# The output product of two attention mixers: native float32 or three rounded products

## The reference

```
def sliding_sink_attention(h, w_in, w_out, sinks, rel_table):
    q, k, v = jnp.split(h @ w_in, [qw, qw + kw], axis=-1)
    ...
    o = banded_attention(q, k, v, rel_table, A_WINDOW, sinks)
    return o.reshape(B, S, -1) @ w_out
```

## Time and profile before

| | |
|---|---|
| median of three runs | 2666.44 us (2665.11 to 2669.57) |
| the profiled execution | 2662.52 us, of which the span of the trace is 2660.7 |
| PE busy | 2609.0 us, 98% of the span |
| DVE, ACT, POOL busy | 1745.3, 1293.1, 241.9 us |
| first mixer A, steps 0 to 9 | from 239.0 to 291.3 us |
| fourth mixer A, steps 0 to 9 | from 1778.7 to 1831.0 us |
| granted PE clock | 0.99 over the span, 1.00 in both mixers A |

### The profile page before, as it was taken

How to read it: one execution, slowest core, us unless ns; L and a number is a source line. 1 busy time by engine, 2 the same in 40 slices (tenths; PEclk the granted TensorE clock), 3 DMA queues, 4 the chain that set the end, 5 groups by cost and what they waited for, 6 DMA issues and landing times.

```text
span 2660.7 us, 37977 instructions
## 1 busy us (share of the span) xinstructions
PE 2609.0 (98%) x13576; PEld 2103.9 (79%) x13576; DVE 1745.3 (66%) x2589; ACT 1293.1 (49%) x2041; POOL 241.9 (9%) x364
## 2 busy tenths in 40 slices
PE   8999999999998999999999999999999999899999
PEld 7887688888874788888988888886888654688887
DVE  6764577777674777777567777745776542577776
ACT  5444454544544544545565454435443221466665
POOL 0001100100111100101110010012001001000000
PEclk9999999999998999999999999999999999999999
DMA  9542555454332555453355545434553222478885
GB/s 321 193 148 87 180 207 189 153 204 179 116 115 82 219 191 192 151 189 141 135 183 215 192 169 190 158 135 150 194 197 132 95 95 71 178 276 287 302 299 191
DMA packets 337248, 472.40 MB, mean 178 GB/s; under 512 B 15632, under 2 KB 275056, under 8 KB 337152
## 3 DMA queue, kind: packets, MB, share of 16 engines
q1 hardware_dynamic: 334464, 464.02, 48.9%
q0 software_dynamic: 2192, 6.94, 0.8%
q10 hardware_dynamic: 496, 0.17, 0.0%
HBM read 470.01 MB, written 1.10 MB: 177 GB/s over the span
## 4 chain that ended last, share of the span: by engine, by line
PE 90%; DVE 5%; ACT 2%; issue 1%; DMA 1%; POOL 0%; SPq 0%; DVEq 0%; ACTq 0%; POOLq 0%
PE psum_all L1456 22%; PE psum_all L1460 12%; PE psum_all L1508 6%; PE psum_all L1509 6%; PE psum_all L1510 6%; PE psum_all L1593 4%; PE psum_all L2455 4%; PE psum_all L1718 3%; PE psum_all L3396 3%; PE psum_all L3415 3%; PE psum_all L3392 3%; PE psum_all L3393 2%; PE psum_all L1635 2%; PE psum_all L3420 1%; PE psum_all L2577 1%
## 5 line engine op out<-in xcount | busy, mean ns | idle before, releaser
L1456 PE MATMUL psum_all<-hT_both,gu_hi 128*128 128x512 f32 x2688 | 670.8, 391 | 0.3 <-DVE gu_lo L1286 0.3
L1456 PEld LDWEIGHTS psum_all<-hT_both,gu_hi 128*128 128x128 f32 x2688 | 492.8, 188 | 95.5 <-DVE gu_lo L1286 0.6
L1286 DVE TENSOR_TENSOR gu_lo<-raw_ring,gu_hi 128x2048 fp32r<-128x2048 f32 x176 | 402.1, 2286 | 15.1 <-ACT gu_hi L1274 9.6
L1460 PEld LDWEIGHTS psum_all<-hT_both,gu_lo 128*128 128x128 f32 x2688 | 366.7, 190 | 26.2
L1460 PE MATMUL psum_all<-hT_both,gu_lo 128*128 128x256 f32 x2688 | 374.8, 282 | 0.0
L1274 ACT ACTIVATE gu_hi<-raw_ring 128x2048 fp32r (+1 forms) x175 | 334.1, 1912 | 16.5 <-DVE oT L1982 8.1
L1281 ACT ACTIVATE down_hi<-raw_ring 128x1024 fp32r (+1 forms) x240 | 250.7, 1057 | 137.7 <-PE psum_all L1510 107.5
L1293 DVE TENSOR_TENSOR down_lo<-raw_ring,down_hi 128x1024 fp32r<-128x1024 f32 x240 | 292.5, 1219 | 34.4 <-ACT down_hi L1281 34.4
L1508 PE MATMUL psum_all<-down_hi,hidden_hi 128*128 128x512 f32 x704 | 277.2, 394 | 5.0 <-DVE hidden_lo L1384 4.3
L1509 PE MATMUL psum_all<-down_lo,hidden_hi 128*128 128x512 f32 x704 | 275.9, 392 | 0.0
L1510 PE MATMUL psum_all<-down_hi,hidden_lo 128*128 128x512 f32 x704 | 274.0, 389 | 0.0
(11 more groups left out here) (490 smaller groups left out, 4079.1 us busy)
## 6 DMA issues: line engine op xcount, KB each, us to landing
raw_ring<-in_ffn_w_in SPq DMA_DIRECT2D x174, 1024.0 KB, 7.1
raw_ring<-in_w SPq DMA_DIRECT2D x96, 1024.0 KB, 7.8
raw_ring<-in_ffn_w_out SPq DMA_DIRECT2D x88, 1024.0 KB, 9.1
raw_ring<-in_c_w_in SPq DMA_DIRECT2D x12, 768.0 KB, 5.2
raw_ring<-in_w_in SPq DMA_DIRECT2D x10, 768.0 KB, 6.3
gain<-in_norm_g POOLq DMA_DIRECT2D x12, 512.0 KB, 4.1
raw_ring<-in_a_w_in SPq DMA_DIRECT2D x8, 768.0 KB, 5.2
raw_ring<-in_b_w_in SPq DMA_DIRECT2D x8, 768.0 KB, 5.0
```

Source lines behind the costliest of these rows:

```text
L1286: K.nc.vector.tensor_tensor(K.gu_lo[:, t, :, :], raw_gu(K, slot, t), K.gu_hi[:, t, :, :].bitcast(F32), ALU.subtract).then_inc(K.sem.gu_lo, 1)
L1456: nc.tensor.matmul(out, K.gu_hi[:, t, j, :], K.hT_both[:, k, :, :].rearrange("p c s -> p (c s)"), start=k == 0, stop=False)
L1460: return nc.tensor.matmul(out[:, 0:SEQ], K.gu_lo[:, t, j, :], K.hT_hi[:, k, :], start=False, stop=k == KT - 1)
```

## The change

In the mixers A the output product is made as in C. The projections stay native. ACT rounds the output weights to their high halves in four pieces of 128 x 2048 (steps 0, 1, 3, 4, before the exponentials of the step), into the free tail of the ring slot or into memory that mixer A leaves free (`e0`, `e3`). DVE subtracts for the low halves (steps 0, 1, 3, 5, behind `biased`), in place. For each unit ACT now writes the high half of the result, at the end of its step, and DVE, in place of its copy, the low half, for which it waits for ACT. Twelve fp32r products take the place of four native ones in each of the eight output groups. The functions that C had for this become shared; for C nothing moves.

```
+def rounds_output(b):
+    return b["kind"] in ("A", "C")
...
+            b["wo_place"] = ["tail", "e0", "tail", "e3"]
+            b["rows_high"], b["rows_low"] = {0: [0], 1: [1], 3: [2], 4: [3]}, {0: [0], 1: [1], 3: [2], 5: [3]}
...
+def rounded_output(K, pe, b, c, a, half):
+    pe.wait_ge(K.sem.wo_lo, 4 * b["ro"] + 2 * (c + 1))
+    cols, tok, nc = slice(half * 512, (half + 1) * 512), slice(a * P, (a + 1) * P), K.nc
+    out = K.psum[:, 2 * a + half, :]
+    for r in range(4):
+        _, high, low, _ = rows_views(K, b, 2 * c + r // 2)
+        o_hi, o_lo = (o[:, 4 * c + r, tok] for o in (K.oT_hi, K.oT_lo))
+        nc.tensor.matmul(out, o_hi, high[:, r % 2, cols], start=4 * c + r == 0, stop=False)
+        nc.tensor.matmul(out, o_hi, low[:, r % 2, cols], start=False, stop=False)
+        ins = nc.tensor.matmul(out, o_lo, high[:, r % 2, cols], start=False, stop=4 * c + r == 7)
+    return ins
...
+def act_result_high(K, act, b, x):
+    act.wait_ge(K.sem.oPV, b["unit0"] + x["u"] + 1)
+    K.nc.scalar.activation(result_of(K.oT_hi, x), result_in_psum(K, x), ACT.Copy).then_inc(K.sem.oT_high, 1)
+
+def dve_result_low(K, dve, b, x):
+    dve.wait_ge(K.sem.oPV, b["unit0"] + x["u"] + 1)
+    dve.wait_ge(K.sem.oT_high, 8 * b["ro"] + x["u"] + 1)
+    K.nc.vector.tensor_tensor(result_of(K.oT_lo, x), result_in_psum(K, x), result_of(K.oT_hi, x).bitcast(F32),
+                              ALU.subtract).then_inc(K.sem.oT_sb, 1)
...
@@ dve_mixer, in step j
         if j < len(units) and units[j]["si"] is not None:
             biased(units[j])
+        for c in b["rows_low"].get(j, ()) if rounds_output(b) else ():
+            dve_rows_low(K, dve, b, c)
         for q in b["steps"][j] if j < len(b["steps"]) else ():
             evacuate_turned(q)
-        if j >= behind:
+        if j >= behind and rounds_output(b):
+            dve_result_low(K, dve, b, units[j - behind])
+        elif j >= behind:
             copy_out(units[j - behind])
...
@@ act_mixer, in step j
         if j >= 2:
             copy_pT(units[j - 2])
+        for c in b["rows_high"].get(j, ()) if rounds_output(b) else ():
+            act_rows_high(K, act, b, c)
         if j < len(units) and units[j]["si"] is not None:
             exps(units[j])
         for q in b["steps"][j] if j < len(b["steps"]) else ():
             evacuate_tokens(q)
+        if rounds_output(b) and j >= 2:
+            act_result_high(K, act, b, units[j - 2])
```

More of the change, by code:

```diff
@@ L469, in map_mixers @@
         small = at("w_hi_small", [P, KT * 48], start + 17920, F32R)
-        self.w_hi = {"C": dict(e0=second, e1=third, e3=first), "B": dict(e0=first, e1=spare, small=small)}
+        self.w_hi = {"A": dict(e0=second, e3=first), "C": dict(e0=second, e1=third, e3=first), "B": dict(e0=first, e1=spare, small=small)}
         self.oT_hi = halves("oT_hi", self.arena)
@@ L487, in plan @@
         fill = tile = item = unit = sunit = outs = 0
-        split = used = folded = turned = mixers = posts = chunk = 0
+        split = used = folded = turned = mixers = posts = chunk = rounded_outputs = 0
         ev = {"act": 0, "dve": 0}
@@ L516, in plan @@
                 b["loads"], b["items"] = self.mixer_layout(b)
+                if rounds_output(b):
+                    b["ro"] = rounded_outputs
+                    rounded_outputs += 1
                 if splits(b):
@@ L937, in act_rows_high @@
     place = b["wo_place"][c]
-    if place != "tail":
+    if place != "tail" and b["chunks"]:
         users = [y["last"] for y in b["chunks"] if y["place"] == place] or [len(b["items"]) - 1]
@@ L946, in dve_rows_low @@
     raw, high, low, _ = rows_views(K, b, c)
-    dve.wait_ge(K.sem.wo_hi, c + 1)
+    dve.wait_ge(K.sem.wo_hi, 4 * b["ro"] + c + 1)
     K.nc.vector.tensor_tensor(low, raw, high.bitcast(F32), ALU.subtract).then_inc(K.sem.wo_lo, 1)
@@ L1714, in output @@
     def output(c, a, half):
+        if rounds_output(b):
+            return rounded_output(K, pe, b, c, a, half)
         slot = wait_fill(b["wo_fill"] + c)
@@ L1778, in pe_split_mixer @@
     U0, S0, Q0, turn = b["unit0"], b["sunit0"], b["out0"], b["t"]
-    oT_hi, oT_lo = K.oT_hi, K.oT_lo
     rounds = RoundedProducts(K, pe, b)
@@ L1889, in pe_split_mixer, with result_in_psum, result_of @@
             output(1, a, half).then_inc(K.sem.y_done, 1)
+def result_in_psum(K, x):
+    return K.psum[:, 6 + x["u"] % 2, 0:2 * P].rearrange("p (t s) -> p t s", t=2)
+def result_of(oT, x):
+    return oT[:, 2 * x["quad"]:2 * x["quad"] + 2, x["a"] * P:(x["a"] + 1) * P]
+def act_result_high(K, act, b, x):
[6 more added lines that the diff above has]
+                              ALU.subtract).then_inc(K.sem.oT_sb, 1)
 def dve_query_scale(K, dve, b):
@@ L2043, in coefficients @@
         nc.vector.reciprocal(co, d).then_inc(K.sem.coef, 1)
[L2045 to L2053, removed]
     dve_chunk_low(K, dve, b, 2)
@@ L2077, in dve_split_mixer @@
         if j >= behind:
-            copy_out(units[j - behind])
+            dve_result_low(K, dve, b, units[j - behind])
 def act_mixer(K, act, b):
@@ L2171, in copy_pT @@
         nc.scalar.activation(K.PT[:, u % 2, 0:nj, :], K.psum[:, 4:4 + nj, :], ACT.Copy).then_inc(K.sem.pT_sb, 1)
[L2173 to L2178, removed]
     for q in range(b["ahead"]):
@@ L2198, in act_split_mixer @@
         if j >= behind:
-            out_high(units[j - behind])
+            act_result_high(K, act, b, units[j - behind])
         for c in b["rows_in_step"].get(j, ()) if j >= len(units) else ():
```

## The result

The changed kernel takes 2668.7 us (median of 22 runs) beside 2665.36 us (22 runs) for the kernel before: ratio 1.0015, 95% interval 1.0009 to 1.0021, so 4.0 us more (2.4 to 5.6); the two medians themselves lie 3.3 apart. 2670.5 was forecast on a before of 2666.44, 4.1 more. Its profiled execution has a span of 2670.1 and took 2672.25 us.

What follows compares the result with a forecast made beforehand. PE, 98% busy, bounds the kernel now, but the change makes ACT and DVE's loop late. First mixer +1.5, fourth +0.4, clock 2 x 1.1 sum to +4.1 on 2666.44: 2670.5 us, range 2662 to 2677.

Steps and rivals of the forecast that it cites:

- The bound turns over: Mixers A: ACT and DVE's loop becomes late, 12.0 us per two units against PE's 10.0, so PE waits.
- exponentials of unit 1 late: Mixer start: first weight copy waits for its fill, delaying unit 1's exponentials 1.9 us in first mixer, 0.8 in fourth.
- unit 1 to unit 7, clock at 1.00: Loop's pace: 0.68 us more for each of units 3 to 7, less 0.5 at unit 5; 3.2 a mixer.
- behind unit 7's exponentials: Mixer's end: one more split, PE's 0.9 slack used, output groups shorter by 0.57 and 2.95; -3.6 us a mixer.
- clock: PE's two long waits let its clock fall to 1.2 GHz, slowing the first output group; +1.1 us a mixer, between 0 and 2.
- The 0.68 a unit: Loop from step 2 on: result splitting puts ACT's high half and DVE's low half ahead of the factors, net 0.68 us.
- the fourth mixer's fill: First output-weight fill: taken to land 1.1 us earlier in the fourth mixer, giving +0.4 there against +1.5 in the first.
- PE's waits: New PE waits: 2.4 us ahead of unit 3's values, 3.6 ahead of first output group, 1.1 ahead of unit 7's turning.
- the loop has room: Rival: ACT and DVE's loop absorbs the split and PE keeps its gain, 2656; with the half-way case 2662, 9 in 100.
- its 5.2: PE's saving per mixer A from rounded output groups, 5.2 us, if PE were always the one that is late.
- The table load: Rival: ACT's table load takes a second 1.28 us in each mixer, delaying unit 0's exponentials; 2673.1, 2 in 100.
- The clock rival: Low clock lasts through the first output group or falls again under the last groups; +8 typically, 2674.5; 29 in 100.

Runs made afterwards that it cites:

- the change with its clock held: Changed kernel plus 4 and 7 dummy matmuls in PE's two long waits of each mixer A; ratio 1.0003 to the kernel before.
- the regrouped kernel: Changed kernel with both result halves on DVE, weight copies in later steps, and token tile 0's output groups first; ratio 0.9974 to the kernel before.
- both edits, clock held: Changed kernel with both result halves on DVE and later weight copies, plus 2 and 5 dummy matmuls in PE's waits; ratio 0.9973 to the kernel before.
- the change, regrouped: Changed kernel with only the output groups reordered, token tile 0's first; ratio 0.9993 to the kernel before.

## Why the prediction was right

**The bound turns over: right, by its rows.** Terms against what they measured, by the starts of exponentials; the pace and the clock are parted by the kernel of the change with its clock held:

| term, us | forecast, first / fourth | measured |
|---|---|---|
| exponentials of unit 1 late | 1.9 / 0.8 | 1.9 / 1.2 |
| unit 1 to unit 7, clock at 1.00 | 3.2 / 3.2 | 3.1 / 3.0 |
| behind unit 7's exponentials | -3.6 / -3.6 | -3.6 / -3.6 |
| clock | 1.1 / 1.1 | 0.7 / 1.4 |
| sum | +2.6 / +1.5 | +2.1 / +2.0 |

The 0.68 a unit was right to 0.2 us over all units together, the saving of the last four groups to 0.2 (2.95 forecast; from the start of the first to PE's next instruction they took 13.84 before and 11.06 in the change, 2.78 less). The sum of the two mixers is exact (+4.1) only because two errors of 0.5 cancelled.

**Mis-sized: the fourth mixer's fill.** I took it to land 1.1 earlier than the first's, from the 8.4 and 6.6 us of the earlier trace rows; those lie 1.8 apart, and no row gives the 1.1. The copy started 13.43 us behind the mixer's start in the first and 12.78 in the fourth, 0.65 apart, and with the clock held the order was the other way round, 12.22 in the first and 13.15 in the fourth. The landing varies by a microsecond between executions of nearly the same kernel, and the change put it on the path. One execution's landing is no constant.

**Mis-sized: the clock, in each mixer, though not in sum.** Its range, 0 to 2, held. What was wrong is to take it as the same cost for each mixer. In the first the clock fell behind the second wait only (3.46), in the fourth already behind the first (1.94, with 0.50 from 1812 to 1813 us). The prediction's reading that a wait of 2 us brings a fall each time holds for the kernel before (behind its first 20 us all six PE waits of 1.9 us and more are followed by 0.50 within 3 us) and failed in the first mixer, where 2.21 us brought none.

**PE's waits:** 2.4, 3.6 and 1.1 forecast, 2.21, 3.46 and 0.43 in the first mixer. The third was shorter because the slow group had put PE 1.5 behind: with the clock held it was 1.27. Unit 7 was turned at 291.44; the 290.8 of the forecast was without the clock's 1.1. That ACT idles at least 1.7 us ahead of each unit's exponentials is not so for unit 5 (1.14); no weight copy stands there.

**Behind the mixer:** nothing new was late, DVE's first scaling came at 303.64 (303.0 forecast). That this cover is thin showed only when PE got earlier than in the forecast.

**The rivals.** That the loop has room is ruled out: in the change PE kept none of its 5.2, and each part of it came back as the loop was relieved. The table load held ACT once, for 1.28; the Trainium skill, ScalarE: Activation LUTs (What ACT_TABLE_LOAD costs), adds a drain of some 1.38 us, and here too the trace has 0.02 on either side. The clock rival, given 29 in 100, has two branches. The first came in the fourth mixer: the fall from the first wait lasted through nearly the whole first group, which took 5.16 us, 2.2 more than with the clock held. The mixer's cost was 1.4, only 0.3 more than the 1.1 of the sum. The second, a fall under the last groups, did not come in the changed kernel, whose last wait was 0.43 and 0.32, nor with the clock held, where it was 1.27 and 1.15. In the regrouped kernel it came, behind waits of 0.59 and 1.11, at 1.5 and 1.6 a mixer. So the mechanism exists; that the short last wait is what spared the change is not shown.

## What to carry to other kernels

When PE is busy 98% of the time, compare its step with the loop of the engines beside it before crediting a saving on PE: here 11.15 against 10.64 left half a microsecond of room, and the 1.36 put into the loop turned a saving into a loss. An operation split over two engines is paid where the second waits for the first, so keep both halves on the one that has cover, and give PE's remaining waits work that needs fewer results. A copy that waits for a transfer must not stand ahead of the loop's first instruction.

## What the runs showed of the hardware

**A wait of the same length may or may not let the clock fall.** In one execution the same 2.54 us were followed by 1.00 in the first mixer and 0.50 in the fourth, and in the fourth mixer of the change 1.94 us were followed by 0.50 where 2.21 in the first were not. Waits of 0.59 and 1.11 with a little work between them were followed by 0.50 in both mixers of the regrouped kernel, and waits of 0.69 and 1.11 in the same places by 1.00 in the first mixer of the change, regrouped (0.72 and 1.11 in its fourth, 1.00 too). What decides between them no run here shows. The five waits of 3.4 to 3.5 us that began at 1.00 were all followed by 0.50. The Trainium skill, TensorE: Matmul & The Clock Gate (Why this matters for your kernels), advises to have no idle gap above about 3 us; here gaps well below that were enough at times, and the rows decide. In the six mixers A with dummy matmuls the clock stayed at 1.00 throughout, and so it did in the two where an output group took the place of the last wait.

**Blocks that nobody touched vary by it.** Mixer B, between the fifth and sixth write of `rstd_rows`, has the same instructions in all twelve kernels and took 188.55 us before, 188.99 in the change, and from 185.85 to 190.82 in the experiments. The last blocks, the same stretch before and after:

```profile
2050.00:2100.00 50.00, 50.00 (x215) 1.00 0.40 137
...
2300.00:2400.00 100.00, 95.30 (x424) 0.97 0.76 272
```

```profile
2050.00:2100.00 50.00, 50.00 (x223) 0.97 0.40 137
...
2300.00:2400.00 100.00, 95.66 (x428) 0.95 0.75 269
```

Here the changed kernel's execution lost another 5 us. That is why 4 us can't be read from two spans: the lengths of the touched blocks gave the terms, and the many timed runs the sum. Two kernels whose mixers are 4.3 shorter are 7 us faster by their ratios (both edits, clock held; both edits, regrouped); whether mixers A that end earlier bring the later blocks less of these falls stays open.
